# Gated delta rule of a two-block kernel: 64x64 levels, and one head's state walk placed beside the next head's levels

## What is computed

```python
# q, k: l2norm(silu(conv4(.))), q also * 128**-0.5; v: silu(conv4(.)); log_a, beta: [T, H]
b = jnp.cumsum(gc, axis=-1)                          # per chunk
decay = exp(where(causal, b_i - b_j, -inf))
m = eye + where(strict, beta_i * (k k^T) * decay, 0)
u, w = solve_unit_lower(m, [v * beta, k * (beta * exp(b))])
qk = (q k^T) * decay;  q_dec = q * exp(b);  k_dec = k * exp(b_last - b);  a_last = exp(b_last)
def step(state, ...):                                # over the chunks
    v_new = u_i - w_i @ state
    o = qd_i @ state + qk_i @ v_new
    state = al_i * state + kd_i^T @ v_new
```

## Time and profile before

| | us |
|---|---|
| median of 3 runs (lowest, highest) | 4843.05 (4841.41, 4851.26) |
| profiled execution | 4846.77 |
| its span | 4844.6 |
| TensorE busy | 4411.0 (91%) |
| VectorE busy | 2167.5 (45%) |
| ScalarE busy | 1705.0 (35%) |
| GpSimd busy | 626.4 (13%) |

### The profile page before, as it was taken

How to read it: one execution, slowest core, us unless ns; L and a number is a source line. 1 busy time by engine, 2 the same in 40 slices (tenths; PEclk the granted TensorE clock), 3 DMA queues, 4 the chain that set the end, 5 groups by cost and what they waited for, 6 DMA issues and landing times. The chain is left out here.

```text
span 4844.6 us, 62669 instructions
## 1 busy us (share of the span) xinstructions
PE 4411.0 (91%) x24845; PEld 3463.2 (71%) x24845; DVE 2167.5 (45%) x2869; ACT 1705.0 (35%) x3133; POOL 626.4 (13%) x750
## 2 busy tenths in 40 slices
PE   7999889799979899999999996887688879999999
PEld 2887667588757678888888884654577764788887
DVE  1414777541577531111110102876777748333333
ACT  1312555331365431111111114775554422333222
POOL 0101200110300010001002002764011101000000
PEclk9999899999999999999999997998899999999999
DMA  7435311343321133222322221222111018323322
GB/s 267 140 116 183 123 38 46 113 139 111 124 95 51 59 116 104 93 96 89 104 96 97 92 80 65 63 76 85 61 36 36 18 40 342 107 98 113 121 97 78
DMA packets 250894, 485.21 MB, mean 100 GB/s; under 512 B 33064, under 2 KB 73224, under 8 KB 250268
## 3 DMA queue, kind: packets, MB, share of 16 engines
q1 hardware_dynamic: 250656, 481.96, 29.0%
HBM read 360.78 MB, written 121.13 MB: 99 GB/s over the span
## 5 line engine op out<-in xcount | busy, mean ns | idle before, releaser
L484 DVE TENSOR_TENSOR p_wl<-p_raw,p_wh 128x2048 fp32r<-128x2048 f32 x96 | 219.8, 2292 | 1029.1 <-ACT p_wh L408 1029.1
L408 ACT CAST p_wh<-p_raw 128x2048 fp32r<-128x2048 f32 x96 | 183.1, 1910 | 802.6 <-PE p_ps L316 790.5
L316 PE MATMUL p_ps<-p_wh,him 128*128 128x512 f32 x1024 | 400.2, 391 | 2.8 <-DVE p_wl L484 2.8
L316 PE MATMUL p_ps<-p_wh,lom 128*128 128x512 f32 x1024 | 399.4, 390 | 0.0
L316 PE MATMUL p_ps<-p_wl,him 128*128 128x512 f32 x1024 | 399.3, 390 | 0.0
L316 PE MATMUL p_ps<-p_wh,hi 128*128 128x512 f32 x896 | 352.1, 393 | 5.7 <-DVE p_wl L484 5.7
L412 ACT ACTIVATE p_stg<-p_ps 128x512 f32<-128x512 f32 x224 | 133.7, 598 | 635.4 <-PE p_ps L316 587.1
L316 PE MATMUL p_ps<-p_wl,hi 128*128 128x512 f32 x896 | 350.1, 391 | 0.0
L316 PE MATMUL p_ps<-p_wh,lo 128*128 128x512 f32 x896 | 350.0, 391 | 0.0
L316 PE MATMUL p_ps<-him,p_wh 128*128 128x512 f32 x768 | 298.8, 389 | 0.0
L316 PE MATMUL p_ps<-him,p_wl 128*128 128x512 f32 x768 | 298.8, 389 | 0.0
(11 more groups left out here) (377 smaller groups left out, 9464.3 us busy)
## 6 DMA issues: line engine op xcount, KB each, us to landing
p_raw<-w_in SPq DMA_DIRECT2D x96, 1024.0 KB, 5.9
pn_dram<-p_stg SPq DMA_DIRECT2D x128, 256.0 KB, 2.0
spare<-w_down SPq DMA_DIRECT2D x32, 1024.0 KB, 4.9
spare<-w_up SPq DMA_DIRECT2D x30, 1024.0 KB, 5.4
p_dram<-p_stg SPq DMA_DIRECT2D x112, 256.0 KB, 2.1
m_w<-w_mod SPq DMA_DIRECT2D x12, 2048.0 KB, 12.2
pt_dram<-p_stg SPq DMA_DIRECT2D x96, 256.0 KB, 2.0
z_ogm<-pn_dram SPq DMA_DIRECT2D x48, 512.0 KB, 13.1
```

Of the source, the lines that this page charges most:

```text
L316: mm = pe.matmul(ps[:, u, :], lhsT, rhs, start=(kk == 0 and q == 0), stop=(kk == KD - 1 and q == 2))
L408: act.copy(wh[:, kh], raw[:, kh]).then_inc(s_wh[kh], 1)
L484: dve.tensor_tensor(wl[:, kh], raw[:, kh], wh[:, kh], ALU.subtract).then_inc(s_wl[kh], 1)
```

## The change

The levels work on the two 64x64 diagonal blocks of each chunk up to the sixth level, side by side in the halves of the partitions; the seventh joins them with one product each way. X and Y are 64 columns wide, the result is Y in full size. The first level's mask moves from GpSimd to VectorE, the causal mask on DT and the product er from VectorE to GpSimd. The rows come from a product of the repeated scalar column with the identity, without diagonals. The walk of head h - 1 is written between the steps of the levels of head h on every engine, one chunk a level, with one bank for v_new, one for the state product and one for the outputs; the loop has one round more. Below, loops over heads are shown as lists (conditions at the ends left out).

```diff
@@ buffers, masks, order of SyncE
-    NL = 2 * (LEVELS - 1)
+    NX = 2 * LEVELS - 1
+    NS = NCK - 1
+    TC = CK // 2
+    halves = [slice(d * TC, (d + 1) * TC) for d in range(2)]
...
-        masks = sb("masks", [P, CK])
-        turned = sb("turned", [P, LEVELS + 1, CK])
+        turned = sb("turned", [P, LEVELS, TC])
-        dg = sb("dg", [P, 2, NCK, CK])
+        sq = sb("sq", [P, 2, NCK, CK])
-        vb, kd [P, 2, NCK, CK]; DB, MT [P, 2, NCK, CK]; Ml [P, NCK, CK]
+        vb, kd [P, 3, NCK, CK]; DB, MT [P, NCK, CK]
-        XY = sb("XY", [P, 2, NCK, CK])
-        Pm = sb("Pm", [P, NCK, CK])
+        XY = sb("XY", [P, 2, NCK, TC])
+        Y = sb("Y", [P, 2, NCK, CK])
+        Pm = sb("Pm", [P, NCK, TC])
+        blocks = by_t(ps[:, 4, :])
+        small = lambda hf, n: by_t(ps[:, hf, n * 4 * TC:(n + 1) * 4 * TC])
+        eye = turned[:, LEVELS - 1]
...
                 if h + 2 < H:
                     sp.wait_ge(s["conv"], h + 2)
+                    sp.wait_ge(s["conv_v"], h + 2)
                     load(h + 2)
+                if h >= 2:
+                    stores(h - 2)
+            for h in range(H - 2, H):
                 stores(h)
@@ ScalarE: the loop over heads
+            for h in range(H + 1):
+                take_o(h - 1, 0); tokens_step(h + 1, -2)
+                take_o(h - 1, 1); tokens_step(h + 1, -1), (h + 1, 0), (h + 1, 1)
+                take_o(h - 1, 2); taps(h + 2, (0, 1)); taps(h + 2, (2,))
+                take_o(h - 1, 3); rows(h + 2, 6)
+                take_o(h - 1, 4); norm(h - 2); tokens_step(h + 1, 3)
+                take_o(h - 1, 5); tokens_step(h + 1, 2), (h + 1, 4)
+                take_o(h - 1, 6); tokens_step(h + 1, 5)
+                take_o(h - 1, 7); silu(h + 2, 0); silu(h + 2, 1)
+                act.wait_ge(s["w"], h + 1)
+                act.activation(wT[:], bank2(0), ACT.Copy, scale=-1.0).then_inc(s["w_taken"], 1)
+                silu(h + 2, 2)
@@ GpSimd
-            def first_level(h):
-                pool.wait_ge(s["MT"], h + 1)
-                ...
-                pool.tensor_tensor(Ml[:], MT[:, h % 2], over_c(masks[:]), ALU.mult).then_inc(s["M0"], 1)
+            def causal_decay(g):
+                pool.wait_ge(s["beta_taken"], g + 1)
+                pool.tensor_tensor(DT[:, g % 2], DT[:, g % 2], over_c(causal[:]), ALU.mult).then_inc(s["causal"], 1)
+            def decayed_queries(g):
+                pool.wait_ge(s["eb_rows"], g + 1)
+                pool.wait_ge(s["qT_taken"], g + 1)
+                pool.tensor_tensor(er[:, g % 2], eb[:, g % 2], qkT[:, 0], ALU.mult).then_inc(s["qdec"], 1)
             roots(0)
-            for h in range(H): first_level(h); output_roots(h - 1); roots(h + 1)
+            causal_decay(0)
+            for h in range(H + 1): decayed_queries(h); causal_decay(h + 1); roots(h + 1); output_roots(h - 1)
@@ VectorE
-            def diagonals(g):
-                ...
-                for q in range(2):
-                    e = dve.tensor_tensor(dg[:, q], over_c(C.ident[:]), over_t(sc[:, 3 * q, g]), ALU.mult)
+            def first_level(h):
+                dve.wait_ge(s["P"], LEVELS * h + 1)
+                dve.tensor_tensor(Pm[:], blocks, turned[:, 0].unsqueeze(1).to_broadcast([P, NCK, TC]), ALU.mult).then_inc(s["P_taken"], 1)
+                dve.drain()
+                dve.tensor_tensor(XY[:, 0], eye.unsqueeze(1).to_broadcast([P, NCK, TC]), Pm[:], ALU.subtract)
+            def first_turned(h):
+                dve.tensor_tensor(XY[:, 1], eye..., by_t(ps[:, 0, :]), ALU.subtract).then_inc(s["XY_ready"], 1)
+            def masked(h, lev):
+                if lev < LEVELS - 1:
+                    dve.tensor_tensor(Pm[:], blocks, turned[:, lev]..., ALU.mult).then_inc(s["P_taken"], 1)
+                else:
+                    dve.tensor_scalar(Pm[halves[1]], blocks[halves[1]], -1.0, None, ALU.mult).then_inc(s["P_taken"], 1)
+            def updated(h, lev):
+                for hf in range(2):
+                    if lev < LEVELS - 2:
+                        dve.tensor_tensor(x, x, ps[:, hf, :]..., ALU.subtract)      (128x512)
+                    elif lev == LEVELS - 2:
+                        three subtractions of 64 partitions x 256, two of them into Y
+                    else:
+                        dve.tensor_copy(Y[halves[0], h % 2, four, halves[1]], small(hf, 0)[halves[0]])
+            for h in range(H + 1):
+                first_level(h); take_v(h - 1, 0); query_parts(h); first_turned(h); state(h - 1, 0); beta_products(h + 1, 6)
+                lev 1: masked, take_v, updated, state
+                lev 2: masked, take_v, updated, state
+                lev 3: masked, take_v, square_sums(h + 1), updated, state, conv_qk(h + 2, 0, 1)
+                lev 4: masked, take_v, conv_qk(h + 2, 1, 3), updated, state, normed(h + 1)
+                lev 5: masked, take_v, conv_qk(h + 2, 3, 4), updated, state, conv_qk(h + 2, 4, 5)
+                lev 6: masked, take_v, conv_qk(h + 2, 5, 6), conv_v(h + 2, 1, 2), updated, state, conv_v(h + 2, 2, 3)
+                take_v(h - 1, 7); system(h + 1); conv_v(h + 2, 3, 4)
@@ TensorE
+            def spread_rows(q, g, bank):
+                for c in range(NCK):
+                    mm = pe.matmul(chunk(bank, c), sc[:, q, g, c:c + 1].to_broadcast([P, P]), C.ident[:], start=True, stop=True)
+            def first_level(h):                       (waits for MT)
+                for c in range(NCK):
+                    for r in halves:
+                        mm = pe.matmul(blocks[r, c], MT[r, c, r], C.ident[r, r], start=True, stop=True)
+            def first_turned(h):                      (waits for P_taken and w_taken of the head before)
+                        mm = pe.matmul(by_t(ps[:, 0, :])[r, c], Pm[r, c], C.ident[r, r], start=True, stop=True)
+            def level_products(h, lev):               (per half: waits for XY_ready)
+                        if lev < LEVELS - 1:
+                            for r in halves:
+                                mm = pe.matmul(blocks[r, c], MT[r, c, r], XY[r, 0, c], start=True, stop=True)
+                        else:
+                            mm = pe.matmul(blocks[b, c], MT[a, c, b], XY[a, 0, c], start=True, stop=True)
+            def level_updates(h, lev):                (waits for P_taken)
+                            for r in halves:
+                                pe.matmul(small(hf, 0)[r, c % 4], XY[r, 1, c], Pm[r, c], start=True, stop=True)
+                            for r in halves:
+                                mm = pe.matmul(small(hf, 1)[r, c % 4], Pm[r, c], XY[r, 1, c], start=True, stop=True)
+                        (last level: Pm[b, c] with Y[b, h % 2, c, b] alone)
+            for h in range(H + 1):
+                first_level(h); tokens_step(h, 6); new_values(h - 1, 0); first_turned(h); outputs(h - 1, 0); beta_rows(h + 1, 6)
+                lev 1 to 6: level_products(h, lev); new_values(h - 1, lev); [0 | 2 | rows(h + 2, 6) | - | 3 | 4];
+                            level_updates(h, lev); outputs(h - 1, lev); [lev 1: tokens_step(h + 1, 1)]
+                new_values(h - 1, 7); tokens_step(h + 1, 5); outputs(h - 1, 7)
+                w: eight products kb x Y into banks 0 and 1 (waits for XY_ready and kparts)
```

More of the change, by code:

```diff
@@ L2098, in taps @@
                 act.wait_ge(s["raw"], 48 * (g + 1))
[L2099 to L2102, removed]
+                if g > 0:
+                    act.wait_ge(s["tokens"], 3 * g if 2 in streams else 3 * g - 1)
                 for q in streams:
@@ L2175, in norm, with take_o @@
                 e.then_inc(s["o_normed"], 1)
-            for h in range(H):
+            def take_o(h, c):
+                m = NCK * h + c
+                act.wait_ge(s["o"], m + 1)
+                if c == 0 and h >= 2:
+                    act.wait_ge(s_st[h % 2], 16 * (h // 2))
+                act.activation(junk[:, c % 2], ps[:, 3, 0:CK], ACT.Square, accum_out=so[:, h % 2, c:c + 1])
+                act.copy(o[:, h % 2, c], ps[:, 3, 0:CK]).then_inc(s["o_taken"], 1)
+            taps(0, (0, 1))
@@ new lines, in _ @@
+            taps(0, (2,))
+            gates()
+            for q in (0, 1, 2):
+                silu(0, q)
+            for step in (-2, -1, 1, 0):
+                tokens_step(0, step)
+            rows(0, 0)
+            taps(1, (0, 1))
+            taps(1, (2,))
+            for step in (3, 4):
+                tokens_step(0, step)
+            rows(1, 4)
+            for q in (0, 1, 2):
+                silu(1, q)
+            for step in (2, 5):
+                tokens_step(0, step)
+            for h in range(H + 1):
@@ L2267, in scalars @@
                 dve.drain()
-            def diagonals(g):
-                if g > 0:
-                    dve.wait_ge(s["beta_rows"], g)
-                for q in range(2):
-                    e = dve.tensor_tensor(dg[:, q], over_c(C.ident[:]), over_t(sc[:, 3 * q, g]), ALU.mult)
-                e.then_inc(s["diagonals"], 1)
```

(31 more changed lines are left out.)

436 lines of the change are left out of this document (220 added, 216 removed).

## The result

The changed kernel takes **4703.09 us** (median of 4 runs, 4700.09 to 4703.61), the kernel before 4842.23 beside it (4840.59 to 4851.26): a ratio of 0.971, 95% interval 0.969 to 0.972. The forecast was 4707 with a range of 4675 to 4780. The profiled execution took 4702.96 us.

A forecast was written before the change was run, and what follows sets the result against it. TensorE and VectorE release each other in turn, so levels and walk in series bound a head. Terms 3443+48+254+44+36.3+16.5+8.7 = 3850.5, 136 us less, so 4843 - 136 = 4707 us; range 4675 to 4780.

The forecast's parts named there:

- The sum: Whole kernel: prologue, eight heads, last walk and tail end at 3850.5, so 136 us less and 4707 us.
- the prologue: Work before head 0: 8.4 us of VectorE work leaves, GpSimd holds cost up to 4.7; first head starts 3443 for 3448.2.
- a sign of being wrong: Steady heads: a granted clock below 1.00 was listed among the observations that would show the forecast wrong.
- The steady head: One head in the loop: 50.8 us for 68.3, chain decides until level 3, then VectorE's own queue.
- The sum of 42 us for TensorE: TensorE per head: levels at 20.7 us plus about 21.7 us of unchanged instructions, 42 us in all.
- Small blocks: TensorE's 64x64 products in the levels: 27.5 ns each in diagonal pairs, 55 in one quadrant, 0.14 us per shape change.
- The hold on `eye - Pm`: Start of a head: GpSimd's decayed queries hold this VectorE subtraction, near 2.9 us instead of 0.69, +2.2 on the path.
- Rival 1: Stalls of in-order queues on VectorE, ScalarE and GpSimd: head period 55 to 60 us, 4740 to 4780 us; chance 20%.
- the hand walk: The prediction's step-by-step timing of one steady head from TensorE's first level, waits included, giving 50.8 us.
- Rival 2: TensorE levels: diagonal blocks run one after the other, 55 ns an instruction, some 11 us more a head, 4795; chance 9%.
- Rival 3: TensorE levels: each small instruction costs 90 ns through block-change entries, slower than before at 4923 us; chance 3%.
- Rival 4: Nothing moves because VectorE's total hardly falls; would need a head period of 64.8 us; chance 2%.

The follow-up runs named there:

- exchanged kernel: The changed kernel with GpSimd's two products exchanged, the decayed queries behind the next head's causal product: 4691.88 us.
- The two kernels with extra work: The changed kernel plus two unused 128x1024 VectorE products a head: at level 6 (late) 4720.30 us, at level 1 (early) 4704.00 us.
- the kernel with the blocks apart: The changed kernel with each group of small products going through all upper 64x64 blocks first, then all lower ones: 4766.18 us.
- the walk in series: The changed kernel with the whole walk of head h-1 ahead of head h's levels on TensorE, VectorE and ScalarE: 4776.53 us.
- the kernel with the value taps moved: The kernel with GpSimd's two products exchanged, v's three taps of the next head moved to levels 1 and 2: 4686.71 us.

## Why the prediction was right

**The sum.** Its terms stand against the marks: head 0's first level 3438.5 for 3443, head 0 47.9 for 48, heads 1 to 5 251.7 for 254, head 6 45.0 for 44, head 7's levels 35.9 for 36.3, the last walk 17.0 for 16.5, the tail 8.7 for 8.7. Together 3844.7 for 3850.5. The largest miss, 4.5 us, is the prologue: 1.65 of it is the stage's start (square sums at 3415.95 for 3417.60 before), which moves by itself. The rest is that the effective start was counted from VectorE. In the trace TensorE starts the first level at 3438.50, behind the system alone, and VectorE reaches its mask at 3442.46 after v's taps: 4.0 ahead instead of 1.3. Heads 1 to 5 hide a term that the sum had at nothing: 1.5 and 1.6 us in heads 1 and 5, where the granted clock is 0.97 (50.59 against the 49.05 of the exchanged kernel's heads, not held either, and 51.49 against 49.87). The prediction named such a clock as a sign of being wrong. It was there, and too small to move the sum out of its place.

**The steady head** came out at 49.87 for 50.8, and both halves for the reason given. VectorE ends level 3's updates at 3612.05 + 0.69, 25.9 us into the head (forecast 26.5), and the queue from there to the next first level took 24.0 (forecast 24.3). The two kernels with extra work show that each half has the bound that it was given, but for the last 4.4 us of TensorE. The sizes inside are less exact than the totals. The queue's items as listed add to 22.8 and not 23.7. The sum of 42 us for TensorE isn't its busy time: such a sum gives 51.9 for the kernel before, which is busy 58.7, and after it the trace has 45.4.

**Small blocks.** Slope 29 ns for 27.5, entry 0.14 to 0.15 for 0.14, TensorE's 544 paired instructions thus about 1 us dearer a head and no more. The last level's 16 in one quadrant took 1.07 us for 16 x 0.055 + 0.14 = 1.02. The prices read from the other stage's few rows held here, though the third of them, the 24 instructions without the entry, is (0.75 - 0.14) / 24 = 25 ns and not 27.

**VectorE:** 38.8 us a head for 39; the 64x256 piece 0.414 for 0.42. The 64x512 mask took 0.694 for 0.6: half the partitions bring nothing, the columns count.

**The hold on `eye - Pm`** is the term whose size on the path was off. It was there in six of eight heads (2 to 7), 2.34 us where 2.9 was expected, since GpSimd starts 1.4 us into the head and not 1.9 and the held instruction ends 0.54 after it. The prediction laid 2.2 us on the path; taking it away gave 0.8 a head, because the wait for v_new then takes the rest. In heads 1 to 5 the sum has 11 us for the hold where the runs give 3.3. The clock put 3.1 back and the rest of a head 2.3 (49.05 without a hold, for 48.6), so that these heads came out only 2.3 us under their 254 is in part luck.

**Rival 1** (in-order stalls, 4740 to 4780) fell: in the steady head VectorE finds every v_new ready, waits 0.86 us for the system's product as the hand walk had it, and ScalarE takes no output late enough to hold TensorE. **Rival 2** (blocks one after the other) is what the kernel with the blocks apart runs. Its price of an instruction, 55 ns, lies between the 59 inside a quadrant and the 50 over a group, but its time did not come: 4766 for 4795. It asked 15 us more of TensorE a head and 11 on the path, where TensorE's busy time rose by 9.2 (54.6 for 45.4) and the period by 7.0, since the VectorE half swallows most of the longer groups. As to the mechanism, the change's diagonal blocks write one bank and still start 29 ns apart. The Trainium skill, TensorEngine Tiling (Array Packing), Restrictions and Gotchas, says different row tiles cannot access one PSUM bank at once; for blocks that write different partitions of that bank, these runs don't agree with it. **Rival 3** needed 66 ns an instruction; even the worst order costs 59. **Rival 4** needed a period of 64.8.

**Where the gain came from,** by runs and not by argument: with the walk in series 73 of the 140 us are gone, with the diagonal blocks apart 63. No kernel has both, so whether the two add is open, and both carry some microseconds of a lower granted clock. The masks on GpSimd brought 0 (11 in the exchanged order, of which some 6 are explained), the rows from the repeated column 5, about half of it in the prologue.

## What to carry to other kernels

Split a loop body where the bound changes hands and price each edit in its own half: the same 19.4 us of VectorE work cost 1 to 4 us in one half of a head and 17 to 21 in the other, while the page's shares (TensorE 92%, VectorE 44%) pointed to TensorE alone. Look at the granted clock head by head: where TensorE waits for VectorE near a head's end it can fall, and each such head was 1.5 to 1.6 us longer here. Issue neighbouring small matmuls to different quadrants of the array. Work offloaded to GpSimd must stand beside VectorE instructions that read PSUM: where it stood was worth more than that it was moved.

## What the runs showed of the hardware that was not expected

The hold works both ways, and by these rows it goes in turns. In the kernel with the value taps moved, GpSimd's causal product (3586.39, 2.36 us) ends at 3588.75, and the tap that started at 3587.38 ends 1.08 us behind it, at 3589.83. GpSimd's next product has started meanwhile, at 3588.71, and takes 3.35 us instead of 2.36; it ends at 3592.06, and the tap of 3591.38 again ends 1.08 behind it. So 2.45 and 1.76 us are a wait plus some 1.1 of work: whichever starts second waits for the other's instruction to end, and neither just runs slower. The held `eye - Pm` fits: it ends 0.54 us behind GpSimd's product, and alone it takes 0.69.
